# Hybrid block: tables fetched by the weight queue, decay rows two heads ahead, masked key products, seven gate products among the heads

## What is computed

```
proj = rmsnorm(x, norm_mix_w) @ w_in        # (256, 4112)
q, k, v, z, xbc, dt_raw, gates = split(proj)
attn = gqa_attention(q, k, v, ...)          # 8 heads, 2 key heads, axial rope
xbc  = silu(depthwise conv over 7 tokens)   # 768 channels: xs 512, bm 128, cm 128
dt   = softplus(dt_raw + dt_bias); a = -exp(a_log)
# both directions, 8 heads of 64, 2 groups; a_cum = cumsum(dt * a):
y[i, h] = sum_{j<=i} (cm[i].bm[j]) exp(a_cum[i] - a_cum[j]) dt[j] xs[j, h]
        + sum_{j>=i} (the same with the backward dt and a)  +  d_skip[h] xs[i, h]
ssd  = rmsnorm(y * silu(z), norm_w)
g_attn, g_ssd = split(sigmoid(gates + b_gate))
x = x + (g_attn * (attn @ w_attn_o) + g_ssd * (ssd @ w_ssd_o)) @ w_out
```

## Time and profile before

| | us |
|---|---|
| runs, median of 3 | 2798.98 (2796.22 to 2808.4) |
| profiled execution | 2799.47 |
| its span | 2797.6 |
| TensorE busy | 2672.2 (96%) |
| VectorE busy | 1689.5 (60%) |
| ACT busy | 1211.8 (43%) |
| POOL busy | 249.2 (9%) |
| mean granted clock of TensorE | 0.982 |

### The profile page before, as it was taken

How to read it: one execution, slowest core, us unless ns; L and a number is a source line. 1 busy time by engine, 2 the same in 40 slices (tenths; PEclk the granted TensorE clock), 3 DMA queues, 4 the chain that set the end, 5 groups by cost and what they waited for, 6 DMA issues and landing times.

```text
span 2797.6 us, 38576 instructions
## 1 busy us (share of the span) xinstructions
PE 2672.2 (96%) x14019; PEld 2138.1 (76%) x14019; DVE 1689.5 (60%) x2562; ACT 1211.8 (43%) x1985; POOL 249.2 (9%) x378
## 2 busy tenths in 40 slices
PE   6999999999998999999999999999997899799999
PEld 5887588888774888887768888876885544699988
DVE  5764576776463766763356676655664451577676
ACT  4444444544332544443244454444442221466664
POOL 0001100100110001000110010011002000000000
PEclk9999999999998999999999999999998989899999
DMA  8542455554241554552355545435443211477784
GB/s 298 180 142 95 177 188 182 186 180 163 90 166 47 194 195 165 186 197 105 121 188 189 197 162 185 160 113 188 180 139 118 91 61 67 181 268 269 275 299 168
DMA packets 328512, 472.42 MB, mean 169 GB/s; under 512 B 8944, under 2 KB 266352, under 8 KB 328416
## 3 DMA queue, kind: packets, MB, share of 16 engines
q1 hardware_dynamic: 325120, 462.93, 46.2%
q0 software_dynamic: 2800, 8.04, 1.0%
q10 hardware_dynamic: 496, 0.17, 0.0%
HBM read 470.01 MB, written 1.10 MB: 168 GB/s over the span
## 4 chain that ended last, share of the span: by engine, by line
PE 87%; DVE 6%; ACT 3%; DMA 2%; POOL 1%; issue 1%; ACTq 0%; SPq 0%; DVEq 0%; POOLq 0%
PE psum_all L1222 23%; PE psum_all L1223 12%; PE psum_all L1334 6%; PE psum_all L1261 6%; PE psum_all L1262 5%; PE psum_all L1263 5%; PE psum_all L1410 4%; PE psum_all L1849 3%; PE psum_all L2761 2%; PE psum_all L2762 2%; PE psum_all L2763 2%; PE psum_all L1337 2%; DMA raw_ring<-in_w 1%; PE psum_all L1355 1%; PE psum_all L1374 1%
## 5 line engine op out<-in xcount | busy, mean ns | idle before, releaser
L1222 PE MATMUL psum_all<-hT_both,gu_hi 128*128 128x512 f32 x2816 | 1006.0, 400 | 16.7 <-DVE gu_lo L1065 10.4
L1223 PE MATMUL psum_all<-hT_both,gu_lo 128*128 128x256 f32 x2816 | 790.9, 281 | 0.0
L1222 PEld LDWEIGHTS psum_all<-hT_both,gu_hi 128*128 128x128 f32 x2816 | 530.1, 188 | 149.0 <-DVE gu_lo L1065 11.1
L1223 PEld LDWEIGHTS psum_all<-hT_both,gu_lo 128*128 128x128 f32 x2816 | 532.9, 189 | 6.2
L1065 DVE TENSOR_TENSOR gu_lo<-raw_ring,gu_hi 128x2048 fp32r<-128x2048 f32 x176 | 403.0, 2292 | 15.4 <-ACT gu_hi L1053 15.2
L1053 ACT ACTIVATE gu_hi<-raw_ring 128x2048 fp32r (+1 forms) x176 | 334.3, 1902 | 16.1 <-DVE oT L1546 12.2
L1091 ACT ACTIVATE cross_terms<-psum_all 128x256 f32<-128x256 f32 x176 | 67.4, 383 | 594.9 <-PE psum_all L1223 594.9
L1072 DVE TENSOR_TENSOR down_lo<-raw_ring,down_hi 128x1024 fp32r<-128x1024 f32 x240 | 292.4, 1218 | 24.1 <-ACT down_hi L1060 23.2
L1261 PE MATMUL psum_all<-down_hi,hidden_hi 128*128 128x512 f32 x704 | 277.3, 394 | 11.1 <-DVE hidden_lo L1158 10.4
L1262 PE MATMUL psum_all<-down_lo,hidden_hi 128*128 128x512 f32 x704 | 276.0, 392 | 0.0
L1263 PE MATMUL psum_all<-down_hi,hidden_lo 128*128 128x512 f32 x704 | 274.1, 389 | 0.0
(11 more groups left out here) (374 smaller groups left out, 3831.4 us busy)
## 6 DMA issues: line engine op xcount, KB each, us to landing
raw_ring<-in_ffn_w_in SPq DMA_DIRECT2D x176, 1024.0 KB, 7.0
raw_ring<-in_w SPq DMA_DIRECT2D x96, 1024.0 KB, 7.6
raw_ring<-in_ffn_w_out SPq DMA_DIRECT2D x88, 1024.0 KB, 9.1
raw_ring<-in_c_w_in SPq DMA_DIRECT2D x12, 768.0 KB, 5.4
raw_ring<-in_w_in SPq DMA_DIRECT2D x10, 768.0 KB, 5.4
gain<-in_norm_g POOLq DMA_DIRECT2D x12, 512.0 KB, 4.0
raw_ring<-in_a_w_in SPq DMA_DIRECT2D x8, 768.0 KB, 5.1
raw_ring<-in_b_w_in SPq DMA_DIRECT2D x8, 768.0 KB, 5.0
```

The costliest lines, as they stand in the source:

```text
L1222: nc.tensor.matmul(out, w_hi, K.hT_both[:, k, :, :].rearrange("p c s -> p (c s)"), start=k == 0, stop=False)
L1223: return nc.tensor.matmul(out[:, 0:SEQ], w_lo, K.hT_hi[:, k, :], start=False, stop=k == KT - 1)
```

## The change

1. The tables go from POOL's queue to SP's (`sp_hybrid_tables`), ahead of the hybrid block's first weight fill. They wait for the block before the last one only, since the memory that they use is free by then. The gate's bias row stays on POOL, under a semaphore of its own, and waits for the updated x.
2. Items 0 to 4 get banks 0, 2, 3, 1, 5 (`hybrid_bank`); items 2 to 4 wait for nothing, items 5 and 6 for the evacuation of item q-4, the others for that of q-2 as before.
3. Decay rows, subtractions and exps run two heads ahead instead of one.
4. The masks are applied once, to the key products (`products_of_both`, parts in `h_cb` and `h_cb_part`). `weights(h)` is then one group of four instructions straight into `h_mix` and `h_mix_part`. The two halves where both directions meet are no longer added; `state_out` accumulates them, with three matmuls per output instead of two.
5. Gate items 16 to 22 lie among the heads, 23 in the first unit.

```diff
@@ stream_weights, in SP's list, ahead of the loads of a mixer @@
+            if b["kind"] == "H":
+                sp_hybrid_tables(K, sp, b)
@@ the tables @@
-def pool_hybrid_loads(K, pool, b):
+def sp_hybrid_tables(K, sp, b):
+
     nc, ins = K.nc, K.ins
     if b["n"]:
-        pool.wait_ge(K.sem.y_done, 4 * b["n"])
-    nc.gpsimd.dma_start(K.c2[:, :], ins["consts"][:, C_FIRST:C_H_END]).then_inc(K.sem.h_rows, 16)
-    nc.gpsimd.dma_start(K.bgrow[:, :], ins["b_gate_2"][0:1, :]).then_inc(K.sem.h_rows, 16)
+        sp.wait_ge(K.sem.y_done, 4 * (b["n"] - 1))
+    sp.dma_start(K.c2[:, :], ins["consts"][:, C_FIRST:C_H_END]).then_inc(K.sem.h_rows, 16)
...
+def pool_gate_bias(K, pool, b):
+
+    if b["n"]:
+        pool.wait_ge(K.sem.x_new, 4 * b["n"])
+    K.nc.gpsimd.dma_start(K.bgrow[:, :], K.ins["b_gate_2"][0:1, :]).then_inc(K.sem.h_bias_row, 16)
...
-HEAD_ITEMS = ((14, 15), (16,), (), (17,), (), (18,), (), ())
-UNIT_ITEMS = ((19,), (20,), (21,), (22,), (23,), ())
+HEAD_ITEMS = ((14, 15), (16,), (17,), (18,), (19,), (20,), (21,), (22,))
+UNIT_ITEMS = ((23,), (), (), (), (), ())
+
+
+def hybrid_bank(q):
+
+    return (0, 2, 3, 1, 5)[q] if q < 5 else item_bank(q)
...
@@ pe_hybrid @@
     def project(q):
-        if q >= 3:
+        if q >= 7:
             wait_evac(K, pe, b, q - 2)
+        elif q >= 5:
+            wait_evac(K, pe, b, q - 4)
...
+            for i, n in enumerate((0, 1 + a, 3)):
+                i0, jt = SSD_PARTS[n][2], SSD_PARTS[n][1]
+                ins = nc.tensor.matmul(K.psum[:, 6 + a, h * HD:(h + 1) * HD],
+                                       mixed(K, n, h)[:, a * P - i0:(a + 1) * P - i0],
+                                       K.xtok[:, jt, h * HD:(h + 1) * HD], start=i == 0, stop=i == 2)
...
     decay_rows(0)
     project(13)
+    decay_rows(1)
     for h in range(SSD_H):
-        if h + 1 < SSD_H:
-            decay_rows(h + 1)
+        if h + 2 < SSD_H:
+            decay_rows(h + 2)
...
@@ dve_hybrid @@
     def weights(h):
 
-        g = h // (SSD_H // 2)
         dve.wait_ge(K.sem.h_exp, h + 1)
-        if h:
-            dve.wait_ge(K.sem.h_w_sum, h)
...
         if h >= 2:
             dve.wait_ge(K.sem.h_y, h - 1)
...
+        for n, (way, jt, i0, i1) in enumerate(SSD_PARTS):
+            ins = nc.vector.scalar_tensor_tensor(out=mixed(K, n, h), in0=K.dec[:, h % 2, n, i0:i1],
+                                                 scalar=K.dt[:, jt, way * SSD_H + h:way * SSD_H + h + 1],
+                                                 in1=products_masked(K, n, h // (SSD_H // 2)),
+                                                 op0=ALU.mult, op1=ALU.mult)
+        ins.then_inc(K.sem.h_w_sum, 1)
...
     args(0)
+    args(1)
     for h in range(SSD_H):
-        if h + 1 < SSD_H:
-            args(h + 1)
         weights(h)
+        if h + 2 < SSD_H:
+            dve.wait_ge(K.sem.h_w_sum, h + 1)
+            args(h + 2)
         if h == 1:
             norms()
```

More of the change, by code:

```diff
@@ L226, in __init__ @@
             some("h_yT h_so h_merge2 h_mT_ps h_mT_act h_mT_dve h_zs")
-        self.h_w_sum, = some("h_w_sum")
+        self.h_w_sum, self.h_bias_row = some("h_w_sum h_bias_row")
         self.e_small, self.e_lg, self.e_arg, self.e_exp, self.e_comb = \
@@ L385, in map_memory @@
         o = self.arena + 4 * (4 * 8 * SEQ)
-        self.wgt = at("h_weights", [P, 4, SEQ], o)
+        self.cb_part = at("h_cb_part", [P, 2, 2, P], o)
+        self.mm_part = at("h_mix_part", [P, 2, 2, P], o + 2 * 4 * SEQ)
         self.mm = at("h_mix", [P, 2, NT, SEQ], o + 4 * 4 * SEQ)
@@ L1837, in product @@
     def product(q, k):
-        it, bank = items[q], item_bank(q)
+        it, bank = items[q], hybrid_bank(q)
         slot = wait_fill(it["fill"])
@@ L1903, in state_out @@
         for a in range(NT):
-            for jt in range(NT):
-                ins = nc.tensor.matmul(K.psum[:, 6 + a, h * HD:(h + 1) * HD], K.mm[:, h % 2, jt, a * P:(a + 1) * P],
-                                       K.xtok[:, jt, h * HD:(h + 1) * HD], start=jt == 0, stop=jt == NT - 1)
+            for i, n in enumerate((0, 1 + a, 3)):
[3 more added lines that the diff above has]
+                                       K.xtok[:, jt, h * HD:(h + 1) * HD], start=i == 0, stop=i == 2)
         ins.then_inc(K.sem.h_y, 1)
@@ L2061, in convolve @@
         dve.wait_ge(K.sem.proj, b["item0"] + t + 1)
-        nc.vector.tensor_tensor(K.xbc[:, t, CONV_PAD:CONV_PAD + SEQ], K.psum[:, item_bank(t), 0:SEQ], K.r2_bc[:, :],
+        nc.vector.tensor_tensor(K.xbc[:, t, CONV_PAD:CONV_PAD + SEQ], K.psum[:, hybrid_bank(t), 0:SEQ], K.r2_bc[:, :],
                                 ALU.mult).then_inc(K.sem.evac_dve, 1)
@@ L2108, in args, with products_of_both @@
         ins.then_inc(K.sem.h_arg, 1)
+    def products_of_both():
+        for n, (way, jt, i0, i1) in enumerate(SSD_PARTS):
+            out = K.cb[:, :, n // 2, :] if n in (0, 3) else K.cb_part[:, :, n - 1, :]
+            ins = nc.vector.tensor_tensor(out, K.psum[:, 0:2, jt * SEQ + i0:jt * SEQ + i1],
+                                          tri(K, way, jt, i0, i1).unsqueeze(1).to_broadcast([P, 2, i1 - i0]), ALU.mult)
+        ins.then_inc(K.sem.h_cb, 1)
     def weights(h):
[L2112 removed]
         dve.wait_ge(K.sem.h_exp, h + 1)
[L2114 to L2123 removed]
         if h >= 2:
             dve.wait_ge(K.sem.h_y, h - 1)
[L2126 to L2128 removed]
+        for n, (way, jt, i0, i1) in enumerate(SSD_PARTS):
+            ins = nc.vector.scalar_tensor_tensor(out=mixed(K, n, h), in0=K.dec[:, h % 2, n, i0:i1],
[3 more added lines that the diff above has]
+        ins.then_inc(K.sem.h_w_sum, 1)
     def norms():
@@ L2208, in dve_hybrid @@
     dve.wait_ge(K.sem.h_cb_ps, 1)
-    nc.vector.tensor_copy(K.cb[:, :, :, :].rearrange("p g j i -> p g (j i)"), K.psum[:, 0:2, :]).then_inc(K.sem.h_cb, 1)
+    products_of_both()
     time_steps_rest()
@@ L2274, in evacuate_tokens @@
         act.wait_ge(K.sem.proj, b["item0"] + q + 1)
-        nc.scalar.activation(it["dst"], K.psum[:, item_bank(q), 0:it["n"]], ACT.Silu if it.get("silu") else ACT.Copy,
+        nc.scalar.activation(it["dst"], K.psum[:, hybrid_bank(q), 0:it["n"]], ACT.Silu if it.get("silu") else ACT.Copy,
                              scale=K.st[:, PRE_R + it["a"]:PRE_R + it["a"] + 1]).then_inc(K.sem.evac_act, 1)
@@ L2325, in act_hybrid @@
     evacuate_tokens(13)
+    decays(1)
     for h in range(SSD_H):
-        if h + 1 < SSD_H:
-            decays(h + 1)
+        if h and h + 2 < SSD_H:
+            decays(h + 2)
         for q in HEAD_ITEMS[h]:
```

33 lines of the change are left out of this document (13 added, 20 removed).

## The result

The changed kernel takes 2783.88 us (median of 6 runs, 2779.43 to 2785.13), where the kernel before takes 2805.03 on the same chip (6 runs, 2796.22 to 2810.54). The ratio is 0.9925, with a 95% interval of 0.9908 to 0.9942: 21 us faster, between 16 and 26. In the two profiled executions the spans differ by less, 2797.6 against 2782.1, and the sum in the prediction stands against those.

The account below looks back on a forecast made before the run. TensorE, busy 96% of the span, could give time back only where it idles or runs at a low clock. Tables 10.2 us plus heads and units 6.7 made 16.9 off 2799.47: 2782 as a median, range 2774 to 2794.

Parts of the forecast that it names:

- Part 1: First stage of the hybrid block: earlier tables let VectorE start 13.0 us sooner, of which 10.2 us are gained.
- The term for the clock: Items 7 and 8, behind TensorE's wait of 6.4 us: a low clock loses 2.8 us.
- Part 2: Heads: TensorE never waits, 82.9 us instead of 69.5 with four more gate products; 22.4 us of idling and low clock go.
- Part 3: Attention units: with only product 23 as filler and a falling clock, 41.4 us instead of 62.8.
- The output product: Behind the attention units: the low clock costs about 1.3 us there, between 0.5 and 2.9.
- A: Attention units: the clock holds, which saves 5.3 us, 2777; chance 0.12.
- B: Attention units: product 23 too at 1.2 GHz because a late head still waits, 12.2 us more, 2794; chance 0.20.
- C: First stage: tables or first fill come too late and the tables' gain falls to nothing, 2792; chance 0.05.
- D: SP's queue: column loads ahead of weights make the kernel over 14 us slower, 2813; chance 0.05.

Follow-up runs that it names:

- clock_kept: The change with 13 products that nobody reads in TensorE's wait ahead of item 7; 2780.02 us, ratio 0.9925 against the kernel before.
- one_ahead: The change with decay rows, subtractions and exps one head ahead again instead of two; 2785.37 us, ratio 0.9947 against the kernel before.
- gates_back: The change with its gate products back where they stood before, three in the heads and five in the units; 2770.39 us, ratio 0.9894 against the kernel before.
- sums_back: The change with the heads' old arithmetic: masks per head, halves added on VectorE, two matmuls per output; 2780.15 us, ratio 0.9924 against the kernel before.
- columns_five: The change with 24 further column loads ahead of its own six in the weight queue; 2777.89 us, ratio 0.9919 against the kernel before.
- lead_alone: The kernel before with only decay rows, subtractions and exps moved to two heads ahead; 2783.44 us, ratio 0.9917 against the kernel before.
- banks_back: The change with the old banks and waits of items 0 to 8; 2783.03 us, ratio 0.9941 against the kernel before.
- tables_alone: The kernel before with only the tables moved to SP's queue, bias row still by POOL; 2791.11 us, ratio 0.9964 against the kernel before.
- all_four: The change with gate products back in heads and units, one filling the kT wait, items 7 and 8 in banks 6 and 7, old head arithmetic; 2763.52 us, ratio 0.9857.

## Why the prediction was right, and where it was not

- **The time.** 2782 was forecast and 2783.88 measured, closer than the parts: that is in part luck. The block was forecast 16.9 us shorter, and was 17.6. Against the median of before on this chip, 2805.03, the change gained more, 21; that median was 2798.98 over the first three runs, and 2800 to 2804 on later occasions.
- **Part 1.** 13.0 us for VectorE, a wait of 6.4 us ahead of item 7: measured 12.97 and 6.33. The term for the clock failed in size: I took 2.8, inside bounds of 2.6 to 2.9, from two recoveries of 5.1 and 5.9 us. It was 4.52 (13.44 - 8.92), and clock_kept shows that all of it was the clock's. Behind the same wait the same two items took 11.97 and 11.98 us in one_ahead and gates_back, 13.54 and 13.52 in sums_back and columns_five, so the term is 3.1 to 4.6 us and differs between executions. Two recoveries were too few to bound it. Part 1 gave 8.4 instead of 10.2.
- **Part 2.** Heads 82.9 forecast, 83.02 measured, each term of it within 0.1 us. The sum was right; the reason beside it was not. I wrote that 22.4 us of idling and low clock go, through shorter weights, a further head of lead and work between. Each remedy was taken as needed. The runs show that they overlap: lead_alone removes all but 2.1 us of the waits without the others, one_ahead shows no wait without the lead, sums_back none without the short weights. Whether the gate products alone would do it was not run. What the change does beyond the first remedy is cost: 3.6 us for state products and 11.9 for the gate products.
- **Part 3.** Units 41.4 forecast, 39.95 measured; I had the clock low from one instant to the end, and it came back in between. The output product lost 0.13 instead of 1.3, since the clock rose as it began (window 2308 to 2310). Parts 2 and 3 gave 9.2 instead of 6.7. So two misses of 1.8 and 2.5 us in opposite directions hid each other.
- **The rivals.** A (clock holds in the units) is out by the windows at 2290 and 2300. B (half clock over product 23) did not happen in the profiled execution of the change, where product 23 took 7.13 us, but what it feared is real: with the same instructions product 23 took 9.6 to 9.8 us in banks_back, clock_kept and one_ahead. The reason differs (no wait in a late head, but the 1.91 us for kT), and so does the price: 1.6 us in the units, not 12.2, since the clock was back before the product's end. The windows also bear out what the Trainium skill, "TensorE: Matmul & The Clock Gate", section "A second HAM failure mode: psum-queue depth-cycling", says of short idle times between groups: waits of 1.1 to 2.5 us took the clock to 0.50, let it back to 1.00 and took it down again. C and D did not happen, and columns_five shows that they are further off than priced: five times the column loads do no harm. The Trainium skill, "DMA: Bandwidth & Descriptors", section "SWDGE vs HWDGE vs iDMA", leaves anything irregular to GpSimd, without saying whether a strided load of single words is irregular in its sense. The runs give the price of moving such loads to SP here: 10.61 us of issuing instead of 5.93, at no cost to the block, and 10 us gained by the place in time (tables_alone).
- **What I did not ask.** The prediction summed what TensorE does and never compared two placings of the gate products. Its own numbers held the answer: product 23 alone as filler left 37.4 us at full clock, five products 58.3, so the four that moved cost 20.9 in the units and 32.4 in the heads.

**Left open.** Why the clock comes back after 5 to 6 us in one place and after 9.3 in another, and after 6.4 or 9.3 behind the same wait; why the clock falls behind the same wait of 1.91 us in some executions (units of 41.6 us) and not in others (39.9); why the median of all_four is 5 us over its forecast; what makes a few of the column loads slow to issue.

## What to carry to other kernels

When an in-order engine waits, first ask how early the chain that it waits for could start: moving that start one step ahead cost nothing here (lead_alone), while filler taken from another stage has to be paid there, so compare both stages before moving it. Remedies for one wait don't add up; try each alone. And when a buffer is added so that an engine can run ahead, look at what runs ahead with it (transfers that now collide) and at where it idles instead: several short waits became one of 6.3 us with a low clock behind it.
